# One residual turned between two output tiles: an encoder trunk of two layers with a mixture of experts on one core

## The chip, the core and the metric

The kernel runs on one NeuronCore of a Trainium2 chip. Its engines have one instruction stream each and meet through semaphores: TensorE (PE: matrix products and transposes; PEld is its loading of weights), VectorE (DVE), ScalarE (ACT) and GpSimd (POOL, unused here). SyncE (SP) issues the transfers from HBM into SBUF, the memory that the engines work from; products land in PSUM, which has 8 banks of 512 float32 columns in each of 128 partitions. The metric is the time of one execution on the device in microseconds (us), as the median of several.

## What is computed

```python
x = x + gla_mixer(p, ...) @ w_out                    # the last residual before the experts
...
def moe_swiglu(h, router, w_gate, w_up, w_down):     # h = rms_norm(x, norm2): 256 tokens x 1024
    logits = hf @ router                             # 8 experts
    top_val, top_idx = lax.top_k(logits, 2)
    gates = softmax(top_val)
    ...                                              # tokens sorted by expert, in blocks
    return silu(x_blk @ w_gate[e]) * (x_blk @ w_up[e]) @ w_down[e]   # weighted by gates, added to x
```

Ahead of this stand a layer with two mixers and a dense feed-forward, and the mixer of the second layer. All is float32. A large product is made of three with shorter operands: each operand is split into a high part (`w_high`, `x_high`: a rounded copy, made by ScalarE) and a low part (what is left, by VectorE), and high times high, high times low and low times high are added in PSUM.

## The kernel before

The order of work is written out by hand, as one program for each engine; an engine takes its instructions in that order and waits where the program says `wait_ge(semaphore, count)`. No planner or scheduler decides anything. Weights come through a ring of four slots in SBUF.

The stage of the change has four steps.

1. **Output projection.** `project_out` computes the mixer's output in 8 tiles `j` of 24 products each (lines 156 to 158), two tiles to a PSUM bank, banks 0 to 3, with the features in the partitions. When a pair of tiles is done (`tile_done`), VectorE adds it to the residual `xT` (line 2254, `out_added`); the second pair is added while the sixth tile runs, and the last one right behind the last tile.
2. **Routing.** TensorE multiplies `xT` by the router's matrix (line 2199, 8 products, 16 in the profile's count) and turns `xT` from features by tokens into tokens by features: 16 transposes of 128 x 128 into banks 0 to 3 (`turn_res`, line 2192), a half of the features of one of the two blocks of 128 tokens in each bank. VectorE copies the logits, TensorE turns them (line 2205), VectorE finds the two best experts of each token (lines 2258 to 2266, `chosen`), and TensorE counts each token's rank in its expert (lines 2209 to 2213). `keep_running` (line 289) is a few products on constants that nobody reads.
3. **Splitting the tokens.** Meanwhile ScalarE copies the four banks into `x_res` (line 2226), squares and sums the tokens' rows (2228), makes the scale of the norm with a logarithm and an exponential (2229, 2230) and writes the high part of the scaled tokens, `x_tok_high` (2233). VectorE multiplies the gap between the two best logits by that scale (2269, `gap_ready`); ScalarE takes its exponential (2235). Then ScalarE splits two pieces of the experts' first weights (line 150), loads the table of functions for the experts (2238, `ACT_TABLE_LOAD`) and begins to copy gathered tokens.
4. **Gathering.** VectorE builds `place`, a matrix of ones and zeros that says which token goes to which slot of which expert, in two halves of four experts (`place_slots`, line 2093, two instructions for a half), with the low part `x_tok_low` between the halves (2090). TensorE multiplies the tokens by it (`gather`, line 1874): 16 blocks `i` of four products, the first four with their high halves ahead. The blocks rotate over four banks, so block `i` from the fifth on waits until ScalarE has copied block `i - 4` out (line 2057, `gathered_copied`).

Behind that come 8 experts with 28 groups of weights each, on all engines and on the transfers: the expert stage.

Of the kernel before, what the change touches and what calls it, by code (L numbers as in the profile page):

```python
# [87 lines left out]
def program(nc, io):  # L88
# [13 lines left out]
    with ctx:  # L102
# [1657 lines left out]
        def back_low_part(dve, g, tiles):  # L1760
# [14 lines left out]
        (logits_ready, gap_ready, gap_exp, chosen_ready, ranks1_ready, routed, res_turned) = (  # L1775
            sem(n) for n in ("logits_ready", "gap_ready", "gap_exp", "chosen_ready", "ranks1_ready", "routed",
                             "res_turned"))
        router_gain, logits_t, token_sq, token_rstd = area(misc + 192, KT * E), area(misc + 256, S), area(7680, D), area(misc + 512, 2, TT)
        (router_ready, logits_t_ready, logits_t_copied, token_rstd_ready) = (
            sem(n) for n in ("router_ready", "logits_t_ready", "logits_t_copied", "token_rstd_ready"))  # L1780
# [14 lines left out]
        (x_tok_high, x_tok_ready, gathered_copied, placed, back_turned, back_copied, gathered, slots_high, slots_ready, pair_e_done, silu_e_ready, hidden_e_ready, turned_e,  # L1795
         turned_high, turned_ready, down_e_done, y_high, y_split_ready, scattered, x_added) = (
            sem(n) for n in ("x_tok_high", "x_tok_ready", "gathered_copied", "placed", "back_turned", "back_copied", "gathered", "slots_high", "slots_ready", "pair_e_done",
                             "silu_e_ready", "hidden_e_ready", "turned_e", "turned_high", "turned_ready", "down_e_done", "y_high",
                             "y_split_ready", "scattered", "x_added"))
        TURNS = FET // RING - 1  # L1800
        stored = sem("stored")
# [51 lines left out]
        def moe_products(pe, at):  # L1853
# [13 lines left out]
            def gather(half):  # L1867
# [12 lines left out]
                if first_four:  # L1880
                    pe.wait_ge(x_tok_high, TT)
                for k in first_four:
                    gather_part(k, 0)
                if first_four:
                    pe.wait_ge(x_tok_ready, TT)
                for k in range(KT):
                    i = KT * half + k
                    if i >= 4:
                        pe.wait_ge(gathered_copied, N_GATHERS * p + i - 3)
                        gather_part(k, 0)  # L1890
                    gather_part(k, 1).then_inc(gathered, 1)
# [93 lines left out]
            unit(0, 0, 0, 2)  # L1985
            down(0, 0, 0, first=True)
# [6 lines left out]
        def moe_activations(act, at):  # L1993
# [60 lines left out]
            for i in range(N_GATHERS):  # L2054
# [24 lines left out]

        def place_slots(dve, p):  # L2080
# [4 lines left out]
            for half in range(2):  # L2085
                experts, n = slice(HALF * half, HALF * (half + 1)), HALF
                if half and p == 0:
                    for t in range(TT):
                        dve.wait_ge(x_tok_high, t + 1)
                        nc.vector.scalar_tensor_tensor(x_tok_split[1][:, t], x_res[:, t], token_rstd[:, 1, t:t + 1],  # L2090
                                                       x_tok_split[0][:, t].bitcast(f32), mul, sub).then_inc(x_tok_ready, 1)
# [4 lines left out]
        def moe_elementwise(dve, at):  # L2096
# [74 lines left out]
            dve.wait_ge(scattered, p + 1)  # L2171
            if p:
# [6 lines left out]
        with nc.Block(no_gpsimd_drain=True) as block:  # L2179
# [7 lines left out]
            def _(pe):  # L2187
                project_out(pe, G_OUT1, T_OUT1, 4)
                def turn_res(n):
                    pe.wait_ge(out_added, 8 + 2 * (n // 2) + 2)  # L2190
                    for k in range(4 * (n // 2), 4 * (n // 2) + 4):
                        last = nc.tensor.transpose(ps[n][:, (k % 4) * P:(k % 4 + 1) * P], xT[:, k, (n % 2) * P:(n % 2 + 1) * P], ident)
                    last.then_inc(res_turned, 1)

                pe.wait_ge(router_ready, 1)
                for k in range(KT):
                    if k % 2 == 0:
                        pe.wait_ge(out_added, 8 + k // 2 + 1)
                    last = nc.tensor.matmul(ps[4][0:E, 0:S], router_gain[:, k * E:(k + 1) * E], xT[:, k], start=(k == 0), stop=(k == KT - 1))  # L2199
                last.then_inc(logits_t_ready, 1)  # L2200
                for n in range(4):
                    turn_res(n)
# [6 lines left out]
                nc.tensor.matmul(ps[5][:, 0:E], cst("before"), chosen[:, 0], start=True, stop=True)  # L2209
                nc.tensor.matmul(ps[5][:, E:2 * E], cst("ones"), chosen[:, 0], start=True, stop=False)  # L2210
                nc.tensor.matmul(ps[5][:, E:2 * E], cst("before"), chosen[:, 1], start=False, stop=True)
                nc.tensor.matmul(ps[5][:, 2 * E:3 * E], cst("ones"), chosen[:, 0], start=True, stop=False)
                nc.tensor.matmul(ps[5][:, 2 * E:3 * E], cst("ones"), chosen[:, 1], start=False, stop=True).then_inc(ranks1_ready, 1)
# [4 lines left out]
            def _(act):  # L2218
# [3 lines left out]
                for n in range(2):  # L2222
                    front_high_part(act, G_MOE, n, 0)
                for n in range(4):
                    act.wait_ge(res_turned, n + 1)
                    act_then(act, nc.scalar.activation(x_res[:, n % 2, (n // 2) * 512:(n // 2 + 1) * 512], ps[n][:, :], ACT.Copy))  # L2226
# [192 lines left out]
```

## Time and profile before

| | us |
|---|---|
| median of 3 runs (range) | 1622.71 (1621.55 to 1623.55) |
| the profiled execution, on the device | 1629.35 |
| span of its trace | 1627.6 |
| output projection | 593.94 to 618.69 |
| routing, splitting and gathering | 618.62 to about 643 |
| expert stage | from about 643 to the end |

The profiled execution is 6.64 us above the median, and its span is 1.75 us less than its own time; stages are read from the trace, as distances. Times in rows count from the span's start. The granted clock of TensorE is a share of 2.4 GHz, so 0.50 is the level of 1.2 GHz; a stretch's value is a mean over the two levels.

### The profile page before, as it was taken

The numbers are of one execution on the slowest core, as the hardware profiler recorded it, in microseconds if no ns is written. First come the engines' busy times: TensorE is split into PE (matmuls) and PEld (weight loads), VectorE is DVE, ScalarE is ACT, GpSimd is POOL, SyncE is SP. The second block draws the span as 40 slices with busy tenths as digits, with TensorE's granted clock in tenths as the row PEclk, the third lists the DMA queues.
The fourth block names the chain that finished last, engine by engine and source line by source line (L and its number), as shares of the span: only waits on it lengthen the run. The fifth ranks groups of instructions, "written<-read, shape, count | busy, mean of one in ns | idle before, by whom it ended". The sixth has DMA issues, their size and how long they took to land.

```text
span 1627.6 us, 29965 instructions
## 1 busy us (share of the span) xinstructions
PE 1569.2 (96%) x11044; PEld 1235.2 (76%) x11044; DVE 1258.8 (77%) x1524; ACT 1054.7 (65%) x1425; POOL 0.2 (0%) x4
## 2 busy tenths in 40 slices
PE   7998989999999899999999999999999999999997
PEld 6877878999989778777777777777777777767774
DVE  5876347655556764889889889889899889889885
ACT  4864345443454336777777777777778778777774
POOL 0000000000000000000000000000000000000000
PEclk9999999999999999999999999999999999999999
DMA  8003023554443222899999999999999999999993
GB/s 316 37 1 120 3 80 118 194 193 184 170 163 143 78 80 90 326 372 366 365 369 357 362 378 365 353 373 370 354 367 374 352 371 361 367 368 358 371 369 116
DMA packets 100924, 425.43 MB, mean 261 GB/s; under 512 B 8160, under 2 KB 8160, under 8 KB 95344
## 3 DMA queue, kind: packets, MB, share of 16 engines
q1 hardware_dynamic: 100848, 424.38, 69.6%
q8 instruction: 52, 0.85, 0.2%
q14 instruction: 24, 0.20, 0.0%
HBM read 423.30 MB, written 1.05 MB: 261 GB/s over the span
## 4 chain that ended last, share of the span: by engine, by line
PE 62%; DVE 1%; ACT 0%; issue 0%; DVEq 0%
PE bank L158 20%; PE bank L156 20%; PE bank L157 20%; PE bank L1924 1%; PE bank L1944 1%; PE bank L1874 1%; PE bank L2199 0%; PE bank L1897 0%; ACT xn L2226 0%; DVE x_tok_low L2090 0%; ACT scratch L2228 0%; DVE xn L2177 0%; PE bank L1863 0%; DVE w_low L153 0%; ACT w_high L150 0%
## 5 line engine op out<-in xcount | busy, mean ns | idle before, releaser
L153 DVE TENSOR_TENSOR w_low<-ring,w_high 128x1024 fp32r<-128x1024 f32 x801 | 932.0, 1217 | 45.6 <-ACT w_high L150 45.5
L150 ACT ACTIVATE w_high<-ring 128x1024 fp32r<-128x1024 f32 x801 | 799.8, 1049 | 75.8 <-PE bank L158 55.8
L156 PE MATMUL bank<-w_high,slots_high 128*96 128x512 f32 x448 | 180.3, 402 | 0.0
L156 PE MATMUL bank<-w_high,more_slots_high 128*96 128x512 f32 x448 | 179.5, 401 | 0.0
L158 PE MATMUL bank<-w_high,slots_low 128*96 128x512 f32 x448 | 177.5, 396 | 0.0
L158 PE MATMUL bank<-w_high,more_slots_low 128*96 128x512 f32 x448 | 176.8, 395 | 0.0
L158 PE MATMUL bank<-w_high,turned_low 128*96 128x512 f32 x448 | 176.6, 394 | 0.0
L156 PE MATMUL bank<-w_high,turned_high 128*96 128x512 f32 x448 | 174.9, 390 | 1.1 <-DVE turned_low L153 0.9
L157 PE MATMUL bank<-w_low,turned_high 128*96 128x512 f32 x448 | 175.8, 393 | 0.0
L157 PE MATMUL bank<-w_low,slots_high 128*96 128x512 f32 x448 | 175.8, 392 | 0.0
L157 PE MATMUL bank<-w_low,more_slots_high 128*96 128x512 f32 x448 | 175.4, 391 | 0.0
L156 PE MATMUL bank<-x_high,w_high 128*128 128x256 f32 x416 | 125.2, 301 | 11.4 <-DVE x_low L153 6.9
L2012 ACT ACTIVATE scratch<-bank 96x256 f32<-96x256 f32 x112 | 42.8, 382 | 127.7 <-PE bank L158 127.7
L157 PE MATMUL bank<-x_low,w_high 128*128 128x256 f32 x416 | 121.4, 292 | 0.0
L158 PE MATMUL bank<-x_high,w_low 128*128 128x256 f32 x416 | 121.4, 292 | 0.0
L2121 DVE TENSOR_TENSOR scratch<-scratch,bank 96x256 f32<-96x256 f32 x112 | 46.8, 417 | 79.4 <-ACT scratch L2012 79.4
L156 PE MATMUL bank<-x_gain_high,w_high 128*128 128x256 f32 x352 | 99.9, 284 | 0.6 <-DVE x_gain_low L307 0.6
L157 PE MATMUL bank<-x_gain_low,w_high 128*128 128x256 f32 x352 | 99.6, 283 | 0.0
L158 PE MATMUL bank<-x_gain_high,w_low 128*128 128x256 f32 x352 | 99.6, 283 | 0.0
L156 PEld LDWEIGHTS bank<-w_high,turned_high 128*96 128x96 f32 x448 | 72.4, 162 | 33.0 <-DVE w_low L153 1.6
L156 PEld LDWEIGHTS bank<-x_high,w_high 128*128 128x128 f32 x416 | 83.7, 201 | 17.8 <-issue 11.5
L158 PEld LDWEIGHTS bank<-w_high,slots_low 128*96 128x96 f32 x448 | 72.3, 161 | 31.6
(348 smaller groups left out, 2424.2 us busy)
## 6 DMA issues: line engine op xcount, KB each, us to landing
ring<-in_w_moe SPq DMA_DIRECT2D x224, 1024.0 KB, 6.3
ring<-in_w_moe SPq DMA_DIRECT2D x224, 512.0 KB, 5.9
ring<-in_w_ffn SPq DMA_DIRECT2D x22, 1536.0 KB, 6.6
ring<-in_w_in SPq DMA_DIRECT2D x15, 1536.0 KB, 6.9
ring<-in_w_out SPq DMA_DIRECT2D x6, 1536.0 KB, 7.1
scratch<-in_x SPq DMA_DIRECT2D x2, 512.0 KB, 4.1
out_y<-xn SPq DMA_DIRECT2D x4, 256.0 KB, 2.9
const<-in_const SPq DMA_DIRECT2D x1, 948.0 KB, 13.2
```

The source lines that it names most:

```text
L150: return nc.scalar.activation(dst, src, ACT.Copy)
L153: return nc.vector.tensor_tensor(dst, src, high.bitcast(f32), sub)
L156: nc.tensor.matmul(out, left[0], right[0], start=start, stop=False, **flags)
L157: nc.tensor.matmul(out, left[0], right[1], start=False, stop=False, **flags)
L158: return nc.tensor.matmul(out, left[1], right[0], start=False, stop=stop, **flags)
L1874: last = nc.tensor.matmul(ps[GATHER_BANK[k % 4]][:, 0:HALF * CAP], x_tok_split[n][:, t, k * P:(k + 1) * P], place[:, t, experts].rearrange ...
L1924: last = nc.tensor.transpose(ps[4 + u % 2][:, a * CAP:(a + 1) * CAP], hidden_e[0:CAP, a], ident[0:CAP, 0:CAP])
L1944: last = nc.tensor.matmul(ps[SUM_BANK[2 * half + t]][:, :], back_now[0:CAP, t * P:(t + 1) * P], y_split[n][0:CAP, half * 512:(half + 1) * ...
L2012: nc.scalar.activation(silu_e[0:CAP, :], bank[:, :, 0:P], ACT.Silu).then_inc(silu_e_ready, 1)
L2121: nc.vector.tensor_tensor(hidden_e[0:CAP, :], silu_e[0:CAP, :], two(4 + f // 2 % 2)[0:CAP, :, P:2 * P], mul)\
```

## The change

Half of the transposes and half of the router's products move in front of tile 6 of the output projection (`first_half`), for the features whose sums are already there. The squares are read from the banks of the transposes, one for each half, and their sums are added by VectorE (`sums_ready`). Of the tokens' four parts (half the features of one token block each), the first two are copied to `x_res` early; the other two are split straight from PSUM, and copied to `x_res` later, between ScalarE's copies of gathered blocks 8 and 9, and 11 and 12. The high and low parts are made in four instructions of 512 columns in place of two of 1024. The gap's two instructions on VectorE go behind `place_slots`. Banks change: `TURN_BANK` is 4, 5, 0, 1, the router's bank is 7, the ranks' bank 2.

```diff
-        def project_out(pe, first_group, first_tile, m):
+        def project_out(pe, first_group, first_tile, m, beside=None):
             for j in range(KT):
+                if j == 6:
+                    beside()
...
+                if p == 0 and i in (8, 11):
+                    t = i // 11
+                    act.wait_ge(x_tok_ready, 3 + t)
+                    nc.scalar.activation(x_res[:, t, 512:1024], ps[TURN_BANK[2 + t]][:, :], ACT.Copy).then_inc(x_taken, 1)
...
+        def x_tok_low_part(dve, n):
+
+            t, columns = n % 2, slice(n // 2 * 512, n // 2 * 512 + 512)
+            dve.wait_ge(x_taken, 2 + n + 1)
+            nc.vector.scalar_tensor_tensor(x_tok_split[1][:, t, columns], token_half(n), token_rstd[:, t:t + 1],
+                                           x_tok_split[0][:, t, columns].bitcast(f32), mul, sub).then_inc(x_tok_ready, 1)
...
+                def first_half():
+                    pe.wait_ge(out_added, 8 + 2)
+                    for n in range(2):
+                        turn_res(n, range(4)).then_inc(res_turned, 1)
+                    pe.wait_ge(router_ready, 1)
+                    router_rows(range(4))
+
+                project_out(pe, G_OUT1, T_OUT1, 4, first_half)
+                pe.wait_ge(out_added, 8 + 3)
+                router_rows(range(4, 6))
+                pe.wait_ge(out_added, 8 + 4)
+                router_rows(range(6, 8)).then_inc(logits_ready, 1)
+                for n in (2, 3):
+                    turn_res(n, range(4, 8)).then_inc(res_turned, 1)
                 pe.wait_ge(logits_t_copied, 1)
...
                 nc.vector.tensor_tensor(chosen, hot[:, 0], hot[:, 1], add).then_inc(chosen_ready, 1)
+                dve.wait_ge(part_ready, 4)
+                nc.vector.tensor_tensor(token_part[:, 0], token_part[:, 0], token_part[:, 1], add).then_inc(sums_ready, 1)
+                dve.wait_ge(ranks1_ready, 1)
+                dve_then(dve, nc.vector.tensor_copy(rank.rearrange("p t e -> p (t e)"), ps[2][:, 0:2 * E]))
+                dve_then(dve, nc.vector.tensor_copy(counts, ps[2][:, 2 * E:3 * E]))
+                place_slots(dve, 0)
                 dve_then(dve, nc.vector.tensor_tensor(gap[:, 0], top[:, :, 1], top[:, :, 0], sub))
-                dve.wait_ge(token_rstd_ready, 1)
-                nc.vector.tensor_tensor(gap[:, 0], gap[:, 0], token_rstd[:, 1], mul).then_inc(gap_ready, 1)
-                dve.wait_ge(ranks1_ready, 1)
-                dve_then(dve, nc.vector.tensor_copy(rank.rearrange("p t e -> p (t e)"), ps[5][:, 0:2 * E]))
-                dve_then(dve, nc.vector.tensor_copy(counts, ps[5][:, 2 * E:3 * E]))
-                place_slots(dve, 0)
+                dve.wait_ge(token_scales, 1)
+                nc.vector.tensor_tensor(gap[:, 0], gap[:, 0], token_rstd, mul).then_inc(gap_ready, 1)
```

TensorE at the end of the output projection, before: the last of a tile's products (lines 156 to 158), then all of the router's products (2199) and the first transposes (2192).

```order
L158 MATMUL bank<-x_high,w_low 128x256
L2199 MATMUL bank<-xT,scratch 8x256 [waits out_added,router_ready]
L2199 MATMUL bank<-xT,scratch 8x256
L2199 MATMUL bank<-xT,scratch 8x256 [waits out_added]
L2199 MATMUL bank<-xT,scratch 8x256
L2199 MATMUL bank<-xT,scratch 8x256 [waits out_added]
L2199 MATMUL bank<-xT,scratch 8x256
L2199 MATMUL bank<-xT,scratch 8x256 [waits out_added]
L2199 MATMUL bank<-xT,scratch 8x256
L2192 MATMUL bank<-const,xT 128x128 [waits out_added]
L2192 MATMUL bank<-const,xT 128x128 x3
```

And in the changed kernel, between tile 5 and tile 6:

```order
L158 MATMUL bank<-x_high,w_low 128x256
L2212 MATMUL bank<-const,xT 128x128 [waits out_added]
L2212 MATMUL bank<-const,xT 128x128 x7
L2217 MATMUL bank<-xT,scratch 8x256 [waits router_ready]
L2217 MATMUL bank<-xT,scratch 8x256 x3
L156 MATMUL bank<-x_high,w_high 128x256 [waits front_split]
```

Eight transposes and four of the router's products now stand ahead of the last two tiles; the rest stays behind them, the router's ahead of the transposes as before.

VectorE from the gap to the routing's end, before: the gap's two instructions (2267, 2269), the copies of ranks and counts (2271, 2272), `place_slots` with the low parts in its middle (2082 to 2093), and the largest count (2274).

```order
L2267 TENSOR_TENSOR scratch<-scratch 128x2
L2269 TENSOR_TENSOR scratch<-scratch 128x2 [waits token_rstd_ready,dve_order]
L2271 COPY scratch<-bank 128x16 [waits ranks1_ready]
L2272 COPY scratch<-bank 128x8 [waits dve_order]
L2082 TENSOR_SCALAR scratch<-scratch 128x16 [waits dve_order]
L2083 TENSOR_TENSOR scratch<-scratch 128x16 [waits dve_order]
L2084 TENSOR_SCALAR scratch<-scratch 128x16 [waits dve_order]
L2093 TENSOR_TENSOR place<-const,scratch 128x384 [waits dve_order]
L2093 TENSOR_TENSOR place<-const,scratch 128x384
L2090 SCALAR_TENSOR_TENSOR x_tok_low<-xn,scratch,x_tok_high 128x1024 [waits x_tok_high] x2
L2093 TENSOR_TENSOR place<-const,scratch 128x384 x2
L2274 TENSOR_REDUCE scratch<-scratch 128x1
```

In the changed kernel (2309, 2310 copy ranks and counts, 2312 and 2314 are the gap's instructions):

```order
L2309 COPY scratch<-bank 128x16 [waits ranks1_ready]
L2310 COPY scratch<-bank 128x8 [waits dve_order]
L2105 TENSOR_SCALAR scratch<-scratch 128x16 [waits dve_order]
L2106 TENSOR_TENSOR scratch<-scratch 128x16 [waits dve_order]
L2107 TENSOR_SCALAR scratch<-scratch 128x16 [waits dve_order]
L2114 TENSOR_TENSOR place<-const,scratch 128x384 [waits dve_order]
L2114 TENSOR_TENSOR place<-const,scratch 128x384
L2100 SCALAR_TENSOR_TENSOR x_tok_low<-xn,scratch,x_tok_high 128x512 [waits x_taken] x2
L2100 SCALAR_TENSOR_TENSOR x_tok_low<-bank,scratch,x_tok_high 128x512 [waits x_taken] x2
L2114 TENSOR_TENSOR place<-const,scratch 128x384 x2
L2312 TENSOR_TENSOR scratch<-scratch 128x2
L2314 TENSOR_TENSOR scratch<-scratch 128x2 [waits token_scales,dve_order]
```

The gap's instructions went from the front of `place_slots` to its end, and the low part is in four instructions, two of them from PSUM (`bank`).

ScalarE over the same stretch, before: logarithm and exponential of the norm, high parts, the gap's exponential (2235), two pieces of weights, the table, gathered blocks (2057).

```order
L2229 ACTIVATE scratch<-scratch,param 128x2 [waits act_order]
L2230 ACTIVATE scratch<-scratch 128x2 [waits act_order]
L2233 ACTIVATE x_tok_high<-xn,scratch 128x1024 [waits token_rstd_ready]
L2233 ACTIVATE x_tok_high<-xn,scratch 128x1024
L2235 ACTIVATE scratch<-scratch 128x2 [waits gap_ready]
L150 ACTIVATE w_high<-ring 128x2x512 [waits slot_loaded0]
L150 ACTIVATE w_high<-ring 128x2x512
L2238 ACT_TABLE_LOAD
L2057 ACTIVATE scratch<-bank,param 128x4x96 [waits gathered] x8
```

In the changed kernel (2274 is the gap's exponential, 2065 the gathered blocks):

```order
L2266 ACTIVATE scratch<-scratch,param 128x2 [waits sums_ready]
L2267 ACTIVATE scratch<-scratch 128x2 [waits act_order]
L2271 ACTIVATE x_tok_high<-xn,scratch 128x512 [waits x_taken,token_scales]
L2271 ACTIVATE x_tok_high<-xn,scratch 128x512
L2271 ACTIVATE x_tok_high<-bank,scratch 128x512 x2
L2274 ACTIVATE scratch<-scratch 128x2 [waits gap_ready]
L150 ACTIVATE w_high<-ring 128x2x512 [waits slot_loaded0]
L150 ACTIVATE w_high<-ring 128x2x512
L2277 ACT_TABLE_LOAD
L2065 ACTIVATE scratch<-bank,param 128x4x96 [waits gathered] x8
```

The order on ScalarE is the same but for the shape of the high parts; the exponential still stands ahead of weights, table and gathered blocks, and still waits for `gap_ready`.

## Rows read from the trace of the kernel before

**Rows 1.** The page: busy us of TensorE, share of the span, instructions.

```profile
PE 1569.2 (96%) x11044; PEld 1235.2 (76%) x11044; DVE 1258.8 (77%) x1524; ACT 1054.7 (65%) x1425; POOL 0.2 (0%) x4
```

**Rows 2.** Windows, the expert stage: length, TensorE busy (instructions), granted clock, DMA share, GB/s.

```profile
660.00:1627.00 967.00, 955.30 (x4272) 1.00 0.95 355
```

**Rows 3.** Chain of waits, 586 to 700 us: start, length, what.

```profile
622.87 0.61 ACT xn L2226
...
630.53 2.40 DVE x_tok_low L2090 x2
632.97 10.08 PE bank L1874 x56
```

**Rows 4.** Timeline of TensorE: start, length, line, operation, out<-in, count, [idle before <-releaser].

```profile
618.62 3.62 PE L2199 MATMUL bank<-xT,scratch 128*8 128x256 f32 x16
622.18 1.96 PE L2192 MATMUL bank<-const,xT 128*128 128x128 f32 x16
...
627.98 0.37 PE L2213 MATMUL bank<-scratch,const 128*128 128x8 f32 x2
...
632.97 1.66 PE L1874 MATMUL bank<-place,x_tok_low 128*128 128x384 f32 x8 [0.67 <-DVE x_tok_low L2090]
634.47 0.59 PE L1874 MATMUL bank<-place,x_tok_high 128*128 128x384 f32 x2
```

**Rows 5.** Timeline of ScalarE, 588 to 640 us.

```profile
622.87 2.48 ACT L2226 ACTIVATE xn<-bank 128x512 f32<-128x512 f32 x4 [7.89 <-PE bank L2192]
...
628.31 2.19 ACT L2233 ACTIVATE x_tok_high<-xn,scratch 128x1024 fp32r<-128x1024 f32 x2
630.41 0.19 ACT L2235 ACTIVATE scratch<-scratch 128x2 f32<-128x2 f32 x1
630.50 1.99 ACT L150 ACTIVATE w_high<-ring 128x1024 fp32r<-128x1024 f32 x2
632.51 1.28 ACT L2238 ACT_TABLE_LOAD   x1
633.81 4.32 ACT L2057 ACTIVATE scratch<-bank,param 128x384 f32<-128x384 f32 x8
```

**Rows 6.** Timeline of VectorE, 588 to 640 us.

```profile
626.93 0.15 DVE L2267 TENSOR_TENSOR scratch<-scratch 128x2 f32<-128x2 f32 x1
628.39 0.16 DVE L2269 TENSOR_TENSOR scratch<-scratch 128x2 f32<-128x2 f32 x1 [1.30 <-ACT scratch L2230]
628.47 0.17 DVE L2271 COPY scratch<-bank 128x16 f32<-128x16 f32 x1
...
630.44 2.48 DVE L2090 SCALAR_TENSOR_TENSOR x_tok_low<-xn,scratch,x_tok_high 128x1024 fp32r<-128x1024 f32 x2
632.84 1.02 DVE L2093 TENSOR_TENSOR place<-const,scratch 128x384 fp32r<-128x384 f32 x2
633.77 0.16 DVE L2274 TENSOR_REDUCE scratch<-scratch 128x1 f32<-128x8 f32 x1
```

**Rows 7.** Lines by form, 642 to 1627 us: busy us, mean ns | idle before.

```profile
L2113 DVE SCALAR_TENSOR_TENSOR y_low<-bank,scratch,y_high 96x512 fp32r<-96x512 f32 x16 | 11.2, 742 | 4.8 <-ACT y_high L2003 4.6
```

**Rows 8.** Waits of TensorE, 0 to 600 us: total, times, longest.

```profile
PE bank L156 <- DVE x_low L153: 6.9, 2, 3.5
...
PE bank L156 <- PEq L1598: 2.3, 1, 2.3
```

**Rows 9.** Windows after these waits, and of two later stretches, columns as in the second group.

```profile
22.61:28.84 6.23, 6.23 (x28) 0.50 1.00 424
...
247.25:250.70 3.45, 3.45 (x16) 0.51 0.01 2
...
593.94:598.86 4.92, 4.92 (x29) 0.65 0.81 281
618.62:633.00 14.38, 12.89 (x72) 1.00 0.16 64
652.99:656.96 3.97, 3.97 (x13) 0.57 0.65 238
```

More of the change, by code:

```diff
@@ L1879, in gather @@
                 first_four = range(4) if half == 0 else ()
-                if first_four:
-                    pe.wait_ge(x_tok_high, TT)
+                if first_four and p == 0:
+                    pe.wait_ge(x_taken, 2 + 2)
                 for k in first_four:
                     gather_part(k, 0)
-                if first_four:
-                    pe.wait_ge(x_tok_ready, TT)
+                if first_four and p == 0:
+                    pe.wait_ge(x_tok_ready, 2)
                 for k in range(KT):
@@ L1889, in gather @@
                         pe.wait_ge(gathered_copied, N_GATHERS * p + i - 3)
+                        if i == 4 and p == 0:
+                            pe.wait_ge(x_tok_ready, 4)
                         gather_part(k, 0)
@@ L1985, in moe_products @@
             unit(0, 0, 0, 2)
+            if p == 0:
+                pe.wait_ge(x_taken, 8)
             down(0, 0, 0, first=True)
@@ L2087, in place_slots @@
                 if half and p == 0:
[L2088 to L2091, printed above, removed]
+                    for m in range(4):
+                        x_tok_low_part(dve, m)
                 for t in range(TT):
@@ L2187, in _, with turn_res, router_rows @@
             def _(pe):
[L2188 to L2202, printed above, removed]
+                def turn_res(n, rows):
+                    for k in rows:
+                        last = nc.tensor.transpose(ps[TURN_BANK[n]][:, (k % 4) * P:(k % 4 + 1) * P], xT[:, k, (n % 2) * P:(n % 2 + 1) * P], ident)
+                    return last
+                def router_rows(rows):
+                    for k in rows:
+                        last = nc.tensor.matmul(ps[7][0:E, 0:S], router_gain[:, k * E:(k + 1) * E], xT[:, k], start=(k == 0), stop=(k == KT - 1))
+                    return last
+                def first_half():
[11 more added lines that the diff above has]
+                    turn_res(n, range(4, 8)).then_inc(res_turned, 1)
                 pe.wait_ge(logits_t_copied, 1)
@@ L2208, in _ @@
                 pe.wait_ge(chosen_ready, 1)
[L2209 to L2213, printed above, removed]
+                nc.tensor.matmul(ps[2][:, 0:E], cst("before"), chosen[:, 0], start=True, stop=True)
+                nc.tensor.matmul(ps[2][:, E:2 * E], cst("ones"), chosen[:, 0], start=True, stop=False)
+                nc.tensor.matmul(ps[2][:, E:2 * E], cst("before"), chosen[:, 1], start=False, stop=True)
+                nc.tensor.matmul(ps[2][:, 2 * E:3 * E], cst("ones"), chosen[:, 0], start=True, stop=False)
+                nc.tensor.matmul(ps[2][:, 2 * E:3 * E], cst("ones"), chosen[:, 1], start=False, stop=True).then_inc(ranks1_ready, 1)
                 keep_running(pe, 4, 7)
@@ L2223, in _, with res_square @@
                     front_high_part(act, G_MOE, n, 0)
+                def res_square(n):
+                    act.wait_ge(res_turned, n + 1)
+                    nc.scalar.activation(token_sq[:, n], ps[TURN_BANK[n]][:, :], ACT.Square, accum_out=token_part[:, n // 2, n % 2:n % 2 + 1])\
+                        .then_inc(part_ready, 1)
                 for n in range(4):
[L2225 to L2233 removed]
+                    res_square(n)
+                    if n < 2:
+                        act.wait_ge(part_ready, n + 1)
+                        nc.scalar.activation(x_res[:, n, 0:512], ps[TURN_BANK[n]][:, :], ACT.Copy).then_inc(x_taken, 1)
+                act.wait_ge(sums_ready, 1)
+                act_then(act, nc.scalar.activation(token_rstd, token_part[:, 0], ACT.Ln, scale=1.0 / D, bias=par("eps")))
+                nc.scalar.activation(token_rstd, token_rstd, ACT.Exp, scale=-0.5).then_inc(token_scales, 1)
+                act.wait_ge(token_scales, 1)
+                act.wait_ge(x_taken, 2)
+                for n in range(4):
+                    nc.scalar.activation(x_tok_split[0][:, n % 2, (n // 2) * 512:(n // 2 + 1) * 512], token_half(n), ACT.Copy,
+                                         scale=token_rstd[:, n % 2:n % 2 + 1]).then_inc(x_taken, 1)
                 act.wait_ge(gap_ready, 1)
[L2235 removed]
+                nc.scalar.activation(gap[:, 1], gap[:, 0], ACT.Exp).then_inc(token_scales, 1)
                 for n in range(2):
```

33 lines of the change are left out of this document (15 added, 18 removed).

## The prediction

> **What bounds the kernel now.** I read the page first: TensorE is busy for 96% of the span [rows 1]. The windows of the expert stage come next: 955.3 of its 967 us are TensorE's work, at full clock, with the transfers' engines busy for 95% [rows 2]. So what delays TensorE's entry into that stage moves the end by as much. The stage of the change is read in the chain of waits and in the engines' timelines. The chain leaves TensorE at the last transposes, runs through ScalarE's copies of them, and returns to TensorE from VectorE's low part, which ends at 632.93 [rows 3]. TensorE begins the low products of the gather at 632.97, after 0.67 us of idling, and block 5 (the first whose bank has to be emptied) at 634.47 [rows 4]. ScalarE begins to empty banks at 633.81, the first of eight copies of 0.54 us (4.32 / 8), done at 634.35 [rows 5]; TensorE's eight low products, 0.18 us each (10.08 / 56 [rows 3]), end at 634.4. So two paths arrive within 0.1 us of each other at block 5: VectorE's low part and ScalarE's first copy. A gain needs both to become earlier; a loss needs one to become later.
>
> **TensorE ahead of routing: nothing.** The 8 transposes (half of 1.96 us) and 4 router products (half of 3.62 us) go from behind tile 7 to ahead of tile 6; the same work is done by the time the logits are turned [rows 4]. The last tiles end 2.8 us later and so does the last addition to `xT`, but the two router products that don't need it (a quarter, 0.9 us) cover it: it has 512 columns from PSUM, for which a like instruction takes 0.74 us [rows 7]. Without that cover it would cost its 0.74. The logits are copied later, behind the router's end, and the 8 remaining transposes (1.0 us) cover that. I take 0, at most 0.1 us of delay. VectorE's choice of experts is unchanged.
>
> **The norm becomes earlier, and gains nothing.** The sum of the squares is added on VectorE right behind `chosen`, where the gap's first instruction stood (626.93, 0.15 us), so the logarithm starts near 627.1; before, the norm's result reached VectorE only at 628.39 [rows 6]. The high parts, 2.19 us for two of 1024 columns [rows 5], end near 630 in four pieces. VectorE no longer waits 1.30 us for the norm, but it then waits for the ranks, whose last product ends at 627.98 + 0.37 = 628.35 [rows 4]. The rank copy starts near 628.39 in place of 628.47 [rows 6]: 0.08 us won.
>
> **VectorE up to the gap.** The low part is four instructions of 512 columns in place of two of 1024, which take 1.20 us each and 2.48 in all, so 1.28 with an overlap of 0.08 [rows 3, 6]. On 512 columns from PSUM a like instruction takes 0.742 us [rows 7]; with the same overlap four take 3 x 0.66 + 0.74 = 2.72 us, 0.24 more than before. Bounds: 2.48 (halves cost nothing extra) and 2.97 (no overlap). The second half of `place` starts at 632.84 - 0.08 + 0.24 = 633.00. The gap's subtraction takes the place of the largest count (633.77, 0.16 us [rows 6]): 633.93 to 634.09. A hop of 0.04 (628.35 to 628.39, above) and a multiplication of 0.16 end at 634.29. Then `gap_ready` rises.
>
> **ScalarE behind it, the term that decides.** Before, VectorE's gap came ahead of `place`, and the exponential started at 630.41, as soon as ScalarE had made the high parts [rows 5]. Now it needs `gap_ready`: 634.29 and a hop of 0.06 make 634.35, 3.94 us later. Queued behind it on ScalarE are two pieces of weights (1.99 us), the table (1.28) and the gather's copies [rows 5], and TensorE's block 5 waits for the first copy. All shift by 3.94: copies from 637.75, block 5 at 638.41. TensorE starts the gather near 630.6, does the first four blocks without a pause (the low part now comes in time, so its 0.67 us of idling are gone) in 16 x 0.18 = 2.9 us, and idles for 4.9 us. **Term: +3.9 us**, between 3.7 (the low part's lower bound) and 4.3 (its upper one, and the 0.1 above).
>
> Could ScalarE get past the wait? The row says no: it was idle for 7.89 us up to 622.87, with the pieces of weights behind it in its program untouched until 630.50 [rows 5]. The Trainium skill ("TensorE: Matmul & The Clock Gate", section "Architectural detail") says that the queues of ScalarE and VectorE are strictly first in, first out, which speaks against this change: by it the sum has +3.9 us, and without it weights and table would run from 630 and the term would be nothing. The trace agrees, with those 7.89 us.
>
> **ScalarE's two extra copies** (512 columns from PSUM, 0.61 us each [rows 3]) stand between the gather's copies. TensorE needs 0.72 us for a block (4 x 0.18), ScalarE 0.54, and four banks lie between: the 1.2 us are hidden, or at most 0.1 shows. If TensorE's blocks were no slower than the copies, all 1.2 would show.
>
> **Transfers.** None is moved. The refill of the ring that waits for VectorE's split of the second expert group comes some 0.5 us later; the transfers' engines are nearly idle then (share 0.16 [rows 9]). Nothing.
>
> **The clock.** After an idle stretch TensorE comes back at 1.2 GHz. Two waits for `x_low` (6.9 us together) and one of 2.3 us [rows 8] are followed by 6.23 us at a granted 0.50, 3.45 at 0.51 and 4.92 at a mean of 0.65 [rows 9]. What is lost is length x (1 - clock): 3.1, 1.7 and 1.7 us. The new wait of 4.9 us is longer than any of these. Bounds 1.7 and 3.1; I take the middle, **+2.4 us**. A slow stretch that is there already, 3.97 us at 0.57 [rows 9], costs 1.7 us; I leave it where it is, and it may fall away or be doubled, 1.7 either way.
>
> **Sum.** +3.9 + 2.4 = +6.3 us. The profiled execution goes from 1629.35 to 1635.7 and its span from 1627.6 to 1633.9. It stands 6.64 us above the median of the runs; I carry the difference over: 1622.7 + 6.3 = 1629.0 us.
>
> **Rivals.**
> - *ScalarE blocked, but the clock costs nothing on balance* (no slow stretch after the wait, or the later one falls away in exchange): +3.9 to +4.6, 1627.0 us. For it: the later stretch of 3.97 us will lie elsewhere against the work. Against: all three restarts shown ran at half clock.
> - *Not slower: ScalarE's copies come in time.* If the exponential ran by 630.4, ScalarE would be as early as before and TensorE could win the 0.67 us that it idled: 1622.0. That needs `gap_ready` by 630.4. But the rank copy cannot start before 628.35, from it to the low part's start are 1.97 us, and the low part (2.4) and 1.0 us of `place` stand ahead of the gap [rows 6].
> - *The delay is absorbed in the expert stage*: 1623. TensorE has 11.7 us of idling there [rows 2] in which lost time could hide. Against: over 224 groups of weights that is 0.05 us each, which is no wait for anything that could come earlier.
> - *Transposes let the clock fall.* Eight transposes now stand among the last tiles. Sixteen of them ran inside a stretch with a granted 1.00 [rows 4, 9], so I add nothing; if they did let it fall, one more slow stretch of 1.7 us would come, 1630.7. The Trainium skill ("TensorE: Matmul & The Clock Gate", section "Part 4: PE-mode transpose") states that they don't count as busy, which is this rival. The stretch at 1.00 speaks against it.
>
> **Chances.** Likeliest case 0.62; clock neutral 0.26; not slower 0.04; absorbed 0.04; transposes 0.04. A measurement of this kernel tells changes of over 0.2%, 3.25 us, from none. The first case and the last are slower by more; of the second I leave 0.02 within it. Slower 0.90, same 0.06 (with the absorbed case), faster 0.04. The range: at the low end 3.7 us with nothing for the clock, less 0.9 for the scatter of the median (the runs differ by 2.0 us): 1625.5. At the high end 4.3 + 3.1 + 1.7, with 0.7 of scatter: 1632.5. Three cases lie in it, with 0.92, of which I allow some for sizes that are off.
>
> **What would show it.** Right: ScalarE idle for about 4 us ahead of the gap's exponential; TensorE idle for about 5 us ahead of block 5, near 633.5 to 638.4, released by ScalarE's first copy of a gathered block, then some microseconds at a granted 0.50; an expert stage as long as before; low parts of about 0.74 us each. Wrong: block 5 before 635; an exponential that starts near 630; the logits turned much later than 624.1; an expert stage that is shorter by microseconds; TensorE at full clock behind its wait.

## The result, and the profile after

The changed kernel takes 1629.07 us (median of 6 runs, 1627.19 to 1629.72). The kernel before took 1622.41 us in the same comparison (6 runs, 1621.29 to 1623.55). The ratio is 1.0038, with a 95% interval of 1.0028 to 1.0048: slower, by 6.66 us between the medians.

The spans of the two profiled executions say the opposite: 1625.4 us after, 1627.6 before. The reason lies ahead of the change. The output projection starts at 593.94 us in the trace before and at 585.66 in the trace after; in the experiments below, whose first stages are unchanged, it starts somewhere in between. The changed kernel's profiled execution, of 1627.19 us, is also the fastest of its six. So stages are compared by distances from one event, the turn of the logits: TensorE's first product of 8 x 8 (line 2205 before, 2236 after), at 624.07 before and at 616.07 after. "Block 5" is the first product of the gather that needs a bank emptied by ScalarE.

| distance, us | before | after | difference |
|---|---|---|---|
| output projection's start to the turn | 30.13 | 30.41 | +0.28 |
| turn to block 5 | 10.40 | 14.30 | +3.90 |
| block 5 to the first expert product | 8.42 | 10.24 | +1.82 |
| first expert product to the end | 984.71 | 984.79 | +0.08 |

The sum is +6.08 us; the 0.6 that is missing to the medians' 6.66 lies inside the interval (4.5 to 7.8 us).

The chain of waits of the changed kernel, against [rows 3]: start, length, what.

```profile
622.36 2.73 DVE x_tok_low L2100 x4
625.09 0.93 DVE place L2114 x2
626.53 1.89 ACT w_high L150 x2
628.44 1.28 ACT L2277
629.74 0.59 ACT scratch L2065
630.37 10.41 PE bank L1878 x48
```

Before, the chain went from the low part straight to TensorE. Now it makes a detour: the low part, the second half of `place`, then ScalarE's weights, its table and its first copy, and only then TensorE. (The view lists the longest pieces; the gap and its exponential, between `place` and the weights, are too short for it.) ScalarE's timeline shows why (columns as in [rows 5]):

```profile
619.12 0.29 ACT L2266 ACTIVATE scratch<-scratch,param 128x2 f32<-128x2 f32 x1 [2.11 <-DVE scratch L2307]
...
620.92 1.24 ACT L2271 ACTIVATE x_tok_high<-bank,scratch 128x512 fp32r<-128x512 f32 x2
626.33 0.20 ACT L2274 ACTIVATE scratch<-scratch 128x2 f32<-128x2 f32 x1 [4.17 <-DVE scratch L2314]
626.44 1.99 ACT L150 ACTIVATE w_high<-ring 128x1024 fp32r<-128x1024 f32 x2
628.44 1.28 ACT L2277 ACT_TABLE_LOAD   x1
629.74 2.00 ACT L2065 ACTIVATE scratch<-bank,param 128x384 f32<-128x384 f32 x4
```

ScalarE has its high parts ready at 622.16, and then idles for 4.17 us. The bracket names what ended the idling: VectorE's line 2314, the gap's multiplication. VectorE's timeline shows that the multiplication stands where the change put it, behind the low parts and the second half of `place`:

```profile
622.36 1.41 DVE L2100 SCALAR_TENSOR_TENSOR x_tok_low<-xn,scratch,x_tok_high 128x512 fp32r<-128x512 f32 x2
623.69 1.40 DVE L2100 SCALAR_TENSOR_TENSOR x_tok_low<-bank,scratch,x_tok_high 128x512 fp32r<-128x512 f32 x2
625.01 1.02 DVE L2114 TENSOR_TENSOR place<-const,scratch 128x384 fp32r<-128x384 f32 x2
625.94 0.15 DVE L2312 TENSOR_TENSOR scratch<-scratch 128x2 f32<-128x2 f32 x1
626.13 0.16 DVE L2314 TENSOR_TENSOR scratch<-scratch 128x2 f32<-128x2 f32 x1
```

And TensorE's timeline, against [rows 4], shows who pays:

```profile
622.50 1.66 PE L1878 MATMUL bank<-place,x_tok_high 128*128 128x384 f32 x8 [0.33 <-DVE place L2114]
624.00 1.55 PE L1878 MATMUL bank<-place,x_tok_low 128*128 128x384 f32 x8
630.37 1.01 PE L1878 MATMUL bank<-place,x_tok_high 128*128 128x384 f32 x2 [4.82 <-ACT scratch L2065]
631.17 0.84 PE L1878 MATMUL bank<-place,x_tok_low 128*128 128x384 f32 x2
...
634.37 0.52 PE L1878 MATMUL bank<-place,x_tok_high 128*128 128x384 f32 x2
```

The old wait for the low part (0.67 us) is gone, as the low products follow the high ones at once. In its place stands one wait of 4.82 us for ScalarE's first copy. Behind it a pair of products takes 0.84 us, and from 634.37 on 0.52. The windows of TensorE give the clock (columns as in [rows 2]):

```profile
585.66:590.50 4.84, 4.84 (x28) 0.65 0.82 282
590.50:604.60 14.10, 14.10 (x119) 1.00 0.55 189
604.60:613.20 8.60, 8.60 (x65) 1.00 0.58 206
...
630.30:634.40 4.10, 4.03 (x13) 0.51 0.62 208
634.40:640.60 6.20, 6.20 (x37) 1.00 0.08 32
651.30:654.80 3.50, 3.50 (x11) 0.52 0.64 211
658.00:1625.40 967.40, 955.04 (x4271) 1.00 0.95 355
```

For 4.10 us behind the wait TensorE ran at 1.2 GHz. The stretches that were there before, at the projection's start and 11 us into the experts' work, are still there; the expert stage is as it was.

### The profile page after: what moved, and what is told of

Read it like the earlier page. It is cut to its first block, busy times and chain, and to the rows that moved or that the text cites. A ratio compares the mean times of both kernels' runs of the same rounds, so it can differ in the third digit from the quotient of the medians.

```text
span 1625.4 us, 29973 instructions
## 1 busy us (share of the span) xinstructions
PE 1564.4 (96%) x11044; PEld 1231.2 (76%) x11044; DVE 1259.3 (77%) x1527; ACT 1054.6 (65%) x1431; POOL 0.2 (0%) x4
## 4 chain that ended last, share of the span: by engine, by line
PE 62%; DVE 1%; ACT 0%; issue 0%; DVEq 0%
PE bank L158 20%; PE bank L156 20%; PE bank L157 20%; PE bank L1930 1%; PE bank L1950 1%; PE bank L1878 1%; PE bank L2217 0%; ACT w_high L150 0%; DVE x_tok_low L2100 0%; PE bank L1903 0%; DVE xn L2199 0%; PE bank L2212 0%; PE bank L1867 0%; DVE place L2114 0%; ACT L2277 0%
```

## The experiments

The theory is that of the prediction: the gap's place on VectorE, behind the low parts, blocks ScalarE's queue, and the clock adds some of its own. Rivals are that something else in the change costs the time (the half of the transposes that moved, the extra copies on ScalarE, the low part's four instructions), and that the clock's share is nothing, or is made up for by the late stretch of 3.5 us. The runs were made in two sets, each with its own runs of the kernel before: a median of 1623.83 us for the first four experiments (23 runs), of 1624.12 for the last three (27 runs). The changed kernel was not run again in them. An interval of 0.001 either way is 1.6 us, so that smaller differences are read from the distances alone, each in one profiled execution:

| kernel | turn to block 5 | block 5 to first expert product | first expert product to end | ratio to before (95%) |
|---|---|---|---|---|
| gap first, rest of the change kept | 10.02 | 8.44 | 984.75 | 1.0001 (0.9991 to 1.0011) |
| late gap alone, in the kernel before | 14.05 | 10.02 | 985.23 | 1.0032 (1.0018 to 1.0045) |
| changed kernel, weights ahead of the gap's exponential | 12.41 | 11.28 | 984.71 | 1.0016 (1.0006 to 1.0027) |
| changed kernel, wait filled with products | 14.29 | 8.45 | 984.58 | 1.0026 (1.0015 to 1.0038) |
| gap first, nothing of the transposes moved | 10.03 | 8.45 | 985.02 | 0.9995 (0.9986 to 1.0004) |
| gap first, weights early | 9.32 | 8.32 | 984.58 | 0.9997 (0.9986 to 1.0007) |
| kernel before, weights early | 10.40 | 8.31 | 984.91 | 0.9998 (0.9989 to 1.0008) |

**1. The gap in front again, all else of the change kept.**

```diff
                 nc.vector.tensor_tensor(token_part[:, 0], token_part[:, 0], token_part[:, 1], add).then_inc(sums_ready, 1)
+                dve_then(dve, nc.vector.tensor_tensor(gap[:, 0], top[:, :, 1], top[:, :, 0], sub))
+                dve.wait_ge(token_scales, 1)
+                nc.vector.tensor_tensor(gap[:, 0], gap[:, 0], token_rstd, mul).then_inc(gap_ready, 1)
...
                 place_slots(dve, 0)
-                dve_then(dve, nc.vector.tensor_tensor(gap[:, 0], top[:, :, 1], top[:, :, 0], sub))
-                dve.wait_ge(token_scales, 1)
-                nc.vector.tensor_tensor(gap[:, 0], gap[:, 0], token_rstd, mul).then_inc(gap_ready, 1)
```

> The changed kernel with one edit undone: the gap's two VectorE instructions stand ahead of place_slots again, behind the sum of the squares. Theory (the late gap holds ScalarE, and ScalarE holds block 5 of the gather): ScalarE's idling of 4.2 us ahead of the exponential goes, block 5 starts about 10.0 us after the turn of the logits (14.3 in the changed kernel, 10.4 before), the first expert product 8.4 us behind block 5 at full clock, and the time is about 1622, 0.4 below the kernel before. Rival (the copies and squares from PSUM, the moved transposes or ScalarE's extra copies cost it): block 5 still comes 13 us or more after the turn, and the time stays above 1627.

It takes 1623.74 us, the same as the kernel before; the 0.4 us that were expected below it are too few to tell. ScalarE's timeline of this kernel:

```profile
623.93 1.24 ACT L2271 ACTIVATE x_tok_high<-bank,scratch 128x512 fp32r<-128x512 f32 x2
625.07 0.20 ACT L2274 ACTIVATE scratch<-scratch 128x2 f32<-128x2 f32 x1
625.17 2.00 ACT L150 ACTIVATE w_high<-ring 128x1024 fp32r<-128x1024 f32 x2
627.18 1.28 ACT L2277 ACT_TABLE_LOAD   x1
628.48 4.30 ACT L2065 ACTIVATE scratch<-bank,param 128x384 f32<-128x384 f32 x8
```

The exponential (line 2274) now follows the high parts without a bracket, so without a wait, and TensorE's wait shrinks to this row of its waits (total, times, longest):

```profile
PE bank L1878 <- ACT scratch L2065: 0.5, 1, 0.5
```

Behind it the clock stays at 1.00, and block 5 to the first expert product is 8.44 us. So the whole loss behind the turn hangs on the place of three lines: without it the turn to the end takes 1003.21 us, against 1003.53 before, and the extra copies and the four low parts show no cost there. (What the moved transposes cost ahead of the turn is read in experiment 5.)

**2. The late gap alone.** The kernel before, with its three lines of the gap moved behind `place_slots`. The scratch of ScalarE's squares lies where `place` lies, and until now the gap's wait for the norm kept `place_slots` behind the squares; so this scratch has another address, the one that it has in the changed kernel and in experiment 1, which isn't slow.

```diff
-        router_gain, logits_t, token_sq, token_rstd = area(misc + 192, KT * E), area(misc + 256, S), area(7680, D), area(misc + 512, 2, TT)
+        router_gain, logits_t, token_sq, token_rstd = area(misc + 192, KT * E), area(misc + 256, S), area(0, D), area(misc + 512, 2, TT)
...
-                dve_then(dve, nc.vector.tensor_tensor(gap[:, 0], top[:, :, 1], top[:, :, 0], sub))
-                dve.wait_ge(token_rstd_ready, 1)
-                nc.vector.tensor_tensor(gap[:, 0], gap[:, 0], token_rstd[:, 1], mul).then_inc(gap_ready, 1)
                 dve.wait_ge(ranks1_ready, 1)
...
                 place_slots(dve, 0)
+                dve_then(dve, nc.vector.tensor_tensor(gap[:, 0], top[:, :, 1], top[:, :, 0], sub))
+                dve.wait_ge(token_rstd_ready, 1)
+                nc.vector.tensor_tensor(gap[:, 0], gap[:, 0], token_rstd[:, 1], mul).then_inc(gap_ready, 1)
```

> The kernel before with only the suspect: the gap's two VectorE instructions go behind place_slots (and the squares' scratch area lies elsewhere). Theory: VectorE's place ends 633.86 us into the profile of before, the exponential starts about 634.2 instead of 630.4, block 5 comes 14.2 us after the turn of the logits, and with a restart at half clock (1.8 us) the time is about 1628. Rival (the gap matters only together with the rest of the change): block 5 at 10.4 us, time 1622.4.

It takes 1629.15 us. ScalarE waits 3.58 us for the gap, and TensorE 3.57 us for the first copy (a row of each one's timeline):

```profile
628.71 0.20 ACT L2235 ACTIVATE scratch<-scratch 128x2 f32<-128x2 f32 x1 [3.58 <-DVE scratch L2273]
632.75 0.62 PE L1874 MATMUL bank<-place,x_tok_high 128*128 128x384 f32 x2 [3.57 <-ACT scratch L2057]
```

From the turn on, this kernel needs 1009.30 us to the end, the changed one 1009.33 and the kernel before 1003.53. Moving the gap is enough to reproduce the whole loss behind the turn, and experiment 1 shows that without it nothing is left. That the two sums meet within 0.03 us is chance: the distance from the first expert product to the end alone differs by 0.44 us between them.

**3. Half of what waits behind the exponential goes ahead of it.** In the changed kernel the two pieces of weights on ScalarE don't need the gap.

```diff
+                for n in range(2):
+                    front_high_part(act, G_MOE + 1, n, 0)
                 act.wait_ge(gap_ready, 1)
                 nc.scalar.activation(gap[:, 1], gap[:, 0], ACT.Exp).then_inc(token_scales, 1)
-                for n in range(2):
-                    front_high_part(act, G_MOE + 1, n, 0)
```

> The changed kernel with ScalarE's two pieces of weights (1.99 us) ahead of the gap's exponential, so that only the exponential and the table stay behind the late gap. Theory (what stands behind the wait counts by its length): block 5 comes 12.4 us after the turn of the logits, 1.9 less than in the changed kernel; TensorE then idles for about 2.9 us instead of 4.8. If that is long enough for a restart at half clock, the time is about 1627.2, if not, 1625.4. Rival (block 5 waits for something of VectorE's): no shift.

Block 5 comes 12.41 us after the turn, 1.89 earlier than in the changed kernel: the weights' 2.00 us, less 0.11 because what follows the exponential starts 0.22 us behind it here and 0.11 there. ScalarE's timeline:

```profile
622.19 2.00 ACT L150 ACTIVATE w_high<-ring 128x1024 fp32r<-128x1024 f32 x2
626.46 0.20 ACT L2276 ACTIVATE scratch<-scratch 128x2 f32<-128x2 f32 x1 [2.27 <-DVE scratch L2314]
```

The weights run while the gap is still missing, because they now stand ahead of the wait, and not because ScalarE passes it. The Trainium skill ("TensorE: Matmul & The Clock Gate", section "Architectural detail") states for ScalarE and VectorE that their queues are strictly first in, first out; the trace agrees for ScalarE, with 4.17 us of idling in the changed kernel, in which the weights behind the wait stayed untouched, and 2.27 here.

In this trace only 0.85 of the 1.89 us arrive at the first expert product (23.69 us after the turn, 24.54 in the changed kernel), since the stretch at half clock is longer although the wait is shorter, 2.92 us. I had not expected this. The windows of TensorE show where the clock fell, for the changed kernel, in its wait (the products' ends at 625.55 and the return at 630.37 bound it):

```profile
626.50:627.50 1.00, 0.00 (x0) 1.00 0.00 0
627.50:628.50 1.00, 0.00 (x0) 0.51 0.00 0
628.50:630.30 1.80, 0.00 (x0) 0.50 0.01 5
```

and for this kernel, in its wait (up to 628.61) and behind it:

```profile
626.60:627.60 1.00, 0.00 (x0) 1.00 0.00 0
627.60:628.60 1.00, 0.00 (x0) 0.68 0.00 0
...
628.60:634.80 6.20, 6.19 (x19) 0.50 0.49 156
```

In both the clock fell while TensorE was still idle, and in both it stayed at 1.2 GHz for about as long: from 627.5 to 634.4 in the changed kernel, 6.9 us, and here from 627.96 (0.68 is a mean of 1.00 up to there and 0.50 behind) to 634.8, 6.8 us. In the changed kernel 2.8 us of it lie in the wait and cost nothing; here it is 0.6 us, and the rest falls on work.

This is one execution, and the runs don't bear its size out. From the projection's start to the end the trace takes 1038.80 us, 5.1 more than the trace of before (1033.66); the median of its runs, 1626.53 us, is 2.7 above that of before, with an interval of 1.0 to 4.4 us. So the typical run loses less than the profiled one, and how much of the 1.89 us it keeps is not shown.

**4. The wait filled.** In the changed kernel, ten products on constants (counted as 20) stand in front of the wait for block 5, so that TensorE isn't idle.

```diff
                     if i >= 4:
+                        if i == 4 and p == 0:
+                            keep_running(pe, 10, 5)
                         pe.wait_ge(gathered_copied, N_GATHERS * p + i - 3)
```

> The changed kernel with 10 products on constants (about 4.4 us of TensorE, read by nobody) between the first four blocks of the gather and block 5, so that TensorE works through the wait. Theory (the idle stretch costs the clock): the distance from block 5 to the first expert product is 8.4 us instead of 10.2, at a granted 1.00; block 5 itself stays at 14.3 us after the turn of the logits; the time is 1.8 us below the changed kernel, about 1627.3. Rival (the gather is slow for another reason, such as ScalarE's two extra copies): still 10.2 us.

TensorE's timeline and its clock behind the wait:

```profile
627.59 4.48 PE L289 MATMUL bank<-const 128*128 128x256 f32 x20
632.57 0.62 PE L1878 MATMUL bank<-place,x_tok_high 128*128 128x384 f32 x2 [0.50 <-ACT scratch L2067]
```
```profile
632.50:641.10 8.60, 8.53 (x49) 1.00 0.36 124
```

Block 5 comes no earlier (14.29 us after the turn), but the clock stays at 1.00, and the first expert product is 8.45 us behind it in place of 10.24. So the clock's share of the change is 1.8 us in these traces, and it can be bought back without touching the wait. The median, 1627.62 us, is near the forecast of 1627.3, but the interval of its ratio overlaps with the changed kernel's (1.0028 to 1.0048), so that the run times alone don't show the 1.8 us. What is left of the loss, 22.74 against 18.82 us to the first expert product, is ScalarE's 3.9.

**5. Is the moved half worth anything, once the gap is first?** As experiment 1, but the transposes and router products stay behind the last tile; the squares and tokens still come from PSUM.

```diff
-                def first_half():
...
-                project_out(pe, G_OUT1, T_OUT1, 4, first_half)
+                project_out(pe, G_OUT1, T_OUT1, 4, lambda: None)
+                pe.wait_ge(router_ready, 1)
+                pe.wait_ge(out_added, 8 + 2)
+                router_rows(range(4))
...
-                for n in (2, 3):
-                    turn_res(n, range(4, 8)).then_inc(res_turned, 1)
+                for n in range(4):
+                    turn_res(n, range(n // 2 * 4, n // 2 * 4 + 4)).then_inc(res_turned, 1)
```

> The kernel with the gap first, and the moved half undone as well: all transposes, squares and router products behind the last tile, parts still straight from PSUM. Theory (the earlier norm only saves what lies on ScalarE between the last square and its first copy of a gathered block): the sum of the squares is ready about 0.3 us after VectorE could add it, the high parts and all behind them come some 0.2 us later, and block 5 starts 10.2 us after the turn of the logits instead of 10.0; the time is 0.2 above that kernel's. Rival (the moved half is worth its own length): block 5 at 11 us or later, time 1 us or more above.

Block 5 is 10.03 us behind the turn, as in experiment 1 and not at 10.2 as expected. Even with all four squares left for later, ScalarE waits for VectorE's sum (its timeline, the norm's logarithm):

```profile
624.35 0.30 ACT L2262 ACTIVATE scratch<-scratch,param 128x2 f32<-128x2 f32 x1 [0.57 <-DVE scratch L2303]
```

The logarithm starts 3.05 us behind the turn with the half moved or not, so moving it makes nothing earlier. It costs a little: from the projection's start to the turn 30.41 us in the changed kernel and 30.40 to 30.42 in the experiments that keep the move, 30.12 to 30.14 in the kernels that don't have it (before, experiments 2, 5 and 7).

**6. The weights' pieces early, and the gap first.** In experiment 1 ScalarE's path still ends 0.5 us late at block 5; its two pieces of weights go into its idle time before the last squares.

```diff
                 for n in range(4):
+                    if n == 2:
+                        act.wait_ge(tile_done, T_OUT1 + KT)
+                        for m in range(2):
+                            front_high_part(act, G_MOE + 1, m, 0)
                     res_square(n)
...
-                for n in range(2):
-                    front_high_part(act, G_MOE + 1, n, 0)
```

> The kernel with the gap first, and ScalarE's two pieces of weights (1.99 us) taken from behind the gap's exponential into its idle 6.6 us ahead of the third square, once tile 7 is done. Theory (with the gap first, ScalarE's queue alone holds block 5, by 0.54 us): the copies start when the first gathered block is there, TensorE does not wait for block 5, which starts 9.4 us after the turn of the logits (10.0 with the gap first, 10.4 before), the first expert product 8.4 us behind it; the time is 1.0 us below the kernel before. Rival (the low part's second half or a bank holds it as well): block 5 at 10.0, time 0.4 below.

ScalarE now waits for TensorE's products and not the other way round:

```profile
627.76 4.39 ACT L2065 ACTIVATE scratch<-bank,param 128x384 f32<-128x384 f32 x8 [0.99 <-PE bank L1878]
```

Block 5 follows the turn by 9.32 us, 1.1 earlier than before, and the end by 1002.22, 1.3 earlier, of which the half that is still moved takes back 0.27 ahead of the turn. Its ratio of 0.9997 to the kernel before doesn't tell that from nothing: this is the best arrangement by the traces, but not one that is measurably faster.

**7. The weights early in the kernel before.**

```diff
+                act.wait_ge(tile_done, T_OUT1 + KT)
+                for n in range(2):
+                    front_high_part(act, G_MOE + 1, n, 0)
                 for n in range(4):
...
-                for n in range(2):
-                    front_high_part(act, G_MOE + 1, n, 0)
```

> The kernel before with only that move of ScalarE's two pieces of weights, ahead of its copies of the transposes. Theory (in the kernel before, VectorE's low part arrives at block 5 together with ScalarE's first copy, so that making ScalarE earlier alone wins nothing): block 5 starts 10.3 to 10.4 us after the turn of the logits, as before, and the time is the same within 0.1 us. Rival (ScalarE alone held it): block 5 about 9.8 us after the turn, time 0.6 below.

Block 5 doesn't move (10.40), though ScalarE now idles for 1.73 us ahead of its first copy (its timeline); TensorE still waits for the low part (a row of its waits):

```profile
627.73 4.39 ACT L2057 ACTIVATE scratch<-bank,param 128x384 f32<-128x384 f32 x8 [1.73 <-PE bank L1874]
```
```profile
PE bank L1874 <- DVE x_tok_low L2090: 0.7, 1, 0.7
```

So two paths did meet at block 5 before: relieving ScalarE alone gains nothing.

## Why the prediction was right

- **The deciding term**, the gap's exponential 3.94 us later, measured 3.92: it stood 6.34 us behind the turn [rows 4, 5], and stands 10.26 behind it (626.33 - 616.07). Block 5 moved by 3.90. Experiments 1 and 2, the gap's place undone and done alone, show that this is the cause. ScalarE's idle time (4.17 us) and TensorE's (4.82, forecast 4.9) are where the prediction put them.
- **The low part**, forecast at 2.72 us for four instructions, took 2.73 in the chain.
- **The norm** is earlier, its logarithm 3.05 us behind the turn, forecast 3.03 (627.1 - 624.07). It gains nothing while the ranks and then the gap are awaited: the rank copy is 4.31 us behind the turn, 4.40 before. With the gap first (experiment 1) it brings 0.38 us at block 5, too little to measure.
- **The clock** was right in kind and mis-sized: +2.4 us taken, 1.82 measured in the one trace of the changed kernel, near the lower bound of 1.7. The working took the length of the stretch at half clock from stretches behind other waits. It left out that a part of the fall can lie inside the wait itself, where it costs nothing; here it was 2.8 us of 6.9. Nor does TensorE come back at 1.2 GHz from every wait: behind 3.57 us it ran at a mean of 0.92 at first (experiment 2), behind 0.54 us at 1.00 (experiment 1). The stretch at 651.30 stayed. The prediction priced it at 1.7 us (here 3.50 x 0.48 = 1.7) and let it count for that much either way, and this is wrong: in experiments 2, 3 and 4 it is gone (a granted 1.00 from 640 to 665 us in 2 and 3), and nothing is gained. In experiment 4 the 23.31 us from the first expert product (641.02) to the second row below are all at a granted 1.00, and two waits of TensorE for VectorE, of 0.59 and 0.64 us, stand in them:

```profile
654.73 0.45 PE L156 MATMUL bank<-w_high,turned_high 128*96 128x512 f32 x1 [0.59 <-DVE turned_low L153]
664.33 0.44 PE L156 MATMUL bank<-w_high,turned_high 128*96 128x512 f32 x1 [0.64 <-DVE turned_low L153]
```

  The changed kernel, at a mean of 0.93, does the same product without a wait and at the same distance, 663.92 - 640.61 = 23.31 us:

```profile
663.92 0.45 PE L156 MATMUL bank<-w_high,turned_high 128*96 128x512 f32 x1
```

- **Ahead of the turn** the term was 0 to 0.1 us and measured 0.28. TensorE's weight loads for the second group of router products did wait for the addition to `xT`, 0.32 us, but the products show no loss by it: they take as long as the first group, which didn't wait for an addition (TensorE's timeline of the changed kernel).

```profile
605.46 1.89 PE L2217 MATMUL bank<-xT,scratch 128*8 128x256 f32 x8
613.22 1.89 PE L2217 MATMUL bank<-xT,scratch 128*8 128x256 f32 x8
```

  From start to start, the 0.28 us are spread over all that was cut in two: the tiles take 24.78 us for 24.68 before, the router's products 3.65 for 3.56, the transposes 1.98 for 1.89. That the move costs this, experiment 5 shows; why, stays open.
- **The extra copies on ScalarE** are hidden: with the gap first, block 5 to the first expert product takes 8.44 us with them, 8.42 without.
- **The rivals.** "The clock costs nothing" falls by experiment 4 (1.8 us by the traces). "Not slower" falls with the exponential at 10.26 us. "Absorbed" falls with the expert stage: 984.79 us against 984.71, so the delay at its entry reaches the end whole. "Transposes let the clock fall" falls with the windows from 590.50 to 613.20, which hold the eight that moved and show 1.00. On this the Trainium skill ("TensorE: Matmul & The Clock Gate", section "Part 4: PE-mode transpose") states that transposes don't count as TensorE being busy in the same way; no run here shows a fall from these eight, which stand between the products of two tiles.

The errors of the two small terms, -0.6 and +0.3 us, partly cancel: the traces show 6.1 us where 6.3 were forecast. That 1629.0 us met 1629.07 more closely than that is luck, since the median of before was 1622.41 us in the comparison and 1622.7 in the forecast, and the medians differ by 6.66 us. The forecast for the profiled execution, 1635.7 us with a span of 1633.9, missed by 8.5 (1627.19 and 1625.4): it took the early stages of one execution for those of another, and they differ by 8.28 us here (593.94 - 585.66).

## What to carry to other kernels

A tiny instruction that signals another engine belongs as early in its queue as its inputs allow: two operations on 128 x 2 elements, moved behind the low parts, cost 5.7 us (3.90 + 1.82), since weights, a table and the copies that free PSUM stood behind the one that waited for them. Before moving work ahead to shorten a path, look for what else that path waits for: the squares were made earlier, and their sum still waited for VectorE. When one engine's delay opens a wait on TensorE, add the clock to the bill, or fill the wait with products on constants.

## What the runs showed of the hardware

- In the profiled executions the clock's cost did not go by the length of the wait: 2.92 us of waiting were followed by 6.2 us of work at a granted 0.50 (experiment 3), 4.82 us by 4.1 at 0.51 (the changed kernel), and 3.57 us (experiment 2) by a clock near full first and then 3.2 us at half, so that none of the fall lay in the wait. With the part inside the wait, the stretches at half clock are 6.8, 6.9 and 3.2 us long. They are one execution each, and by its runs the first is not typical, so no size for another wait follows from them. The windows of experiment 2:

```profile
632.70:634.00 1.30, 1.25 (x7) 0.92 0.00 0
634.00:637.20 3.20, 3.20 (x12) 0.50 0.93 319
```

- What lies ahead of the output projection takes up to 8 us more or less from one execution to another, with the same instructions (up to 585.66 us after and up to 593.94 before). That is more than this change costs, and only distances from an event near the change show it in single traces.
